# The first weight panel behind a norm, four output tiles advanced chunk by chunk

## The chip, the cores and the metric

The kernel runs on one core of a Trainium2 chip, as one program with five instruction streams: TensorE (PE), VectorE (DVE), ScalarE (ACT), GpSimd (POOL) and SyncE (SP), which order themselves by semaphores. The metric is the device time of one execution in microseconds (us). All data are float32. Three runs of the kernel before took 4790.31, 4792.47 and 4794.86 us, median 4792.47 us.

## The reference, cut to what matters

Two models follow each other over 512 tokens of width 1024. The first has two layers; 256 context tokens run beside the 512 in its first layer and in the mixer of its second. The second has two layers, each with a gated MLP ahead of its mixer and one behind.

```
# first model, each layer
h = modulate(rms_norm(x, g0), sh1, sc1);  x = x + gt1 * rms_norm(mixer(h), g1)
h = modulate(rms_norm(x, g2), sh2, sc2);  x = x + gt2 * rms_norm(square(relu(h @ w1)) @ w2, g3)
# second model, each layer
h = x + 0.5 * swiglu(rms_norm(x, f1), ...)
n = rms_norm(h, mix);  h = h + concat(conv, window attention, memory attention) @ w_out
h = h + 0.5 * swiglu(rms_norm(h, f2), ...);  x = rms_norm(h, final)
swiglu(h) = (silu(h @ w1) * (h @ w3)) @ w2
```

## The kernel before, in words

Activations lie transposed, as eight chunks of 128 features by 512 or 768 tokens (X the residual, H the normed input). Weights come as panels of 8 chunks by 512 columns through a ring of slots that SP fills ahead of use. A panel holds four output tiles of 128 features. An output tile of up to 512 tokens is a sum over eight chunks in one PSUM bank: eight matmuls, each of which the trace records as two weight loads and two matmuls ("passes" below). Output tiles rotate through banks 0 to 3: `tile()` on TensorE (L1069) waits until the tile four back has been read (semaphore `tile_free`), and on VectorE (L2155) until the tile is done (`tile_done`). `columns` (L1084) goes output tile by output tile and, inside, chunk by chunk; for its first tile it waits per chunk for `h_act`, ScalarE's signal that this chunk of H is written.

Seven panels stand right behind a norm:

- In the even mixer of the first model (`even_in`, L1172): four column tiles times two token segments, 512 and 256 wide. ScalarE writes each chunk of H from VectorE's row scaling (L1754). VectorE copies the tiles out and pools them (L2247 to L2271).
- In the two MLPs of the first model (`mlp`, L1315), item up 0 0: segments of 384 and 384 tokens in the first layer, one of 512 in the second. ScalarE applies relu (L1870) and VectorE multiplies (L2459).
- In the four gated MLPs of the second model (`swiglu`, L1392), item up 0 0: the panel's four tiles are a1, b1, a2, b2 (w1 and w3 columns by turns). Here H is X times the norm's gains, and the factor 1/rms of each token (`r_row`) is applied to the product instead. TensorE computes the sum of squares as a product with a matrix of ones, `root` (L1341), between the panel's first and second tile. VectorE has added up the squares before (L2489, L2492), and behind it makes the variance (L2497), ScalarE the root (L1878), VectorE the reciprocal (L2501). In the third gated MLP (layer 1, first) `root` sums two rows at once and `enter_second` (L2510) needs two roots and two reciprocals, since the layer's final norm and the next norm are folded together.

VectorE's order in these four MLPs is written out (L2734): the reciprocal, `right_first` (L2591, four sums over H through L2563, for the next panel), `first_up` (L2723), `left_sums` (L2608, L2616 and L2618, on the next panel's weights), then the next panel's unit. `first_up` takes a1 times `r_row` (L2726), waits for ScalarE's sigmoid (L1971), multiplies (L2729), multiplies by b1 (L2730), and does the same for a2, b2. In the first of the four, `tables` (L3021 to L3040, the rotary angles) stands between the two pairs.

The other panels of the MLPs are computed as seven products of half size in place of eight (`seven`, L1367, through L1363). The unit's first and second products need only a free bank and the panel; the third one issued, `product(6)`, waits for `tile_free` and so for `left_second` on VectorE (L2631), which stands behind `left_sums` and behind ScalarE's copy of the first product (L1944).

Of the kernel before, what the change touches and what calls it, by code (L numbers as in the profile page):

```python
# [15 lines left out]
P = 128  # L16
D = 1024
KD = D // P
LAT = 512
CTX = 256  # L20
TOK = LAT + CTX
# [44 lines left out]
def mlp_order(beside):  # L66

    for step, (kind, g) in enumerate(mlp_steps(len(FF1_GROUPS))):
        for part in range(2):
            if beside and step in MOD_STEPS:  # L70
                yield "mod", 2 * (step - MOD_STEPS[0]) + part, 0
            yield kind, g, part
# [220 lines left out]
def build_program(nc, panels, vecs, consts, x_in, c_in, mem_in, pool_w, bias, pos, window_in, out, x_save):  # L293
    npanels = panels.shape[0]
    with ExitStack() as ctx:
# [5 lines left out]
        def sem(name):  # L301
            if name not in sems:
                sems[name] = ctx.enter_context(nc.semaphore(name))
            return sems[name]
# [16 lines left out]
        def area(at, *shape):  # L321
            n = int(np.prod(shape))
            flat = arena[:, at:at + n]
            if len(shape) == 1:
                return flat
            names = " ".join("abcd"[:len(shape)])
            return flat.rearrange(f"p ({names}) -> p {names}", **{"abcd"[i]: s for i, s in enumerate(shape)})
# [3 lines left out]
        X, H, Y = (area(o, KD, TOK) for o in (X0, H0, Y0))  # L331
# [129 lines left out]
        SEG1 = ((0, LAT),)  # L461
# [405 lines left out]
        def counting():  # L867


            n = defaultdict(int)  # L870

            def more(name, k=1):
                n[name] += k
                return n[name]

            def one(name):
                n[name] += 1
                return 1

            return n, more, one  # L880
# [179 lines left out]
        def _(pe):  # L1060
            n, more, one = counting()

            def panel():
                p = n["panel"]
                n["panel"] += 1
                pe.wait_ge(sem(f"panel{SLOT[p]}"), 16 * LOADS[p])
                return ring[SLOT[p]]

            def tile():  # L1069

                if n["tile"] - 3 > 0:
                    pe.wait_ge(sem("tile_free"), n["tile"] - 3)
                n["tile"] += 1
                return ps[:, (n["tile"] - 1) % 4, :]

            def accumulate(dest, left, right, nk=KD, ready=None):

                for k in range(nk):
                    if ready:
                        pe.wait_ge(sem(ready), more(ready))  # L1080
                    ins = pe.matmul(dest, left(k), right(k), start=(k == 0), stop=(k == nk - 1))  # L1081
                ins.then_inc(sem("tile_done"), one("tile_done"))

            def columns(w, ms, src, segs, nk=KD, ready=None):  # L1084
                for m in ms:
                    for a, b in segs:
                        accumulate(tile()[:, 0:b - a], lambda k: w[:, k, m * P:(m + 1) * P],
                                   lambda k: src[:, k, a:b], nk, ready)
                        ready = None

            def rows(w, lo, width, src, tok, cols, ready=None):

                for t in tok:
                    accumulate(tile()[:, 0:width], lambda k: src[:, k, t * P:(t + 1) * P],
                               lambda k: w[:, k, cols:cols + width], KD, ready)
                    ready = None
# [19 lines left out]
            def strips(w):  # L1116

                bank = tile()
                each = KD // STRIPS
                for part in range(each):  # L1120
                    for strip in range(STRIPS):
                        k = strip * each + part
                        ins = pe.matmul(bank[strip * STRIP:(strip + 1) * STRIP, :], silu_c[:, k, :], w[:, k, :],  # L1123
                                        start=(part == 0), stop=(part == each - 1))
                ins.then_inc(sem("tile_done"), one("tile_done"))
# [14 lines left out]
            def mod(i, lo, hi):  # L1140

                for j in range(lo, hi, 2):
                    for _ in range(2):
                        strips(panel())
                    strip_sums(i, 2)
# [24 lines left out]
                row(hi)  # L1170

            def even_in():  # L1172
                columns(panel(), range(4), H, ((0, LAT), (LAT, TOK)), ready="h_act")
                mod(0, 4, 6)
                columns(panel(), range(4), H, SEG2)
                mod(0, 6, 8)
                columns(panel(), range(4), H, SEG2)
                mod(0, 8, 10)
                rows(panel(), 0, 512, H, range(TOK // P), 0)
                mod(0, 10, 12)  # L1180
                pe.wait_ge(sem("const_in"), 16)
                pe.wait_ge(sem("pool_w"), 16)
                for g in range(4):
                    pe.wait_ge(sem("pooled"), more("pooled"))
                    for a, b in SEG2:
                        accumulate(tile()[:, 0:b - a], lambda k: pool_wb[:, g, :], lambda k: Y[:, 4 + g, a:b], 1)
# [128 lines left out]
            def mlp(segs, beside):  # L1315
                ends = {}
                between = None
                for item in mlp_order(beside):
                    kind, g, part = item
                    w = panel()  # L1320
                    if kind == "mod":
                        strips(w)
                        between = lambda: strip_sums(1, 1)
                        continue
                    src = H if kind == "up" else hidden1[g % 2]
                    if kind == "down" and part == 0:
                        pe.wait_ge(sem("half_hidden"), ends[g][0])
                        pe.wait_ge(sem("tile_free"), ends[g][1])
                    fast = cuts(item, FF1_GROUPS, beside)
                    for at, c in enumerate(fast):  # L1330
                        if at == 0 and (part == 0 or item == ("up", 0, 1)):
                            n["right"] += 4
                        seven(w, src, mlp_left, c, beside and item == ("up", 0, 1), between)
                        between = None
                    if not fast:
                        columns(w, range(4), src, segs, KD, "h_act" if kind == "up" else None)
                    if kind == "up":
                        n["half_hidden"] += 4 * len(fast)
                        ends[g] = n["half_hidden"], n["tile"]

            def root(count):  # L1341

                if n["norm"] > 0:
                    pe.wait_ge(sem("var"), n["norm"])
                n["norm"] += count
                for i in range(count):
                    pe.wait_ge(sem("accumulated"), more("accumulated"))
                    ins = pe.matmul(ps[:, 4 + i, :], ones[:, :], acc[i], start=True, stop=True)
                ins.then_inc(sem("summed"), one("summed"))
# [42 lines left out]
            def swiglu(l, which):  # L1392
                ends = {}
                for item in swiglu_order():
                    kind, g, part = item
                    w = panel()
                    if kind == "down" and part == 0:
                        pe.wait_ge(sem("half_hidden"), ends[g][0])
                        pe.wait_ge(sem("tile_free"), ends[g][1])
                    fast = cuts(item, FF2_GROUPS)  # L1400
                    if fast:
                        if part == 0 or item == ("up", 0, 1):
                            n["right"] += 4
                        seven(w, H if kind == "up" else hidden2[g % 2], ffn_left, fast[0])
                        if (which, g, part, kind) == (0, 0, 0, "down"):
                            mem_root()
                    elif kind == "up":
                        columns(w, [0], H, SEG1, KD, "h_act")
                        root(2 if (l, which) == (1, 0) else 1)
                        columns(w, range(1, 4), H, SEG1)  # L1410
                    else:
                        columns(w, range(4), hidden2[g % 2], SEG1, FF2_GROUPS[g])
                    if kind == "up":
                        n["half_hidden"] += 4 * len(fast)
                        ends[g] = n["half_hidden"], n["tile"]
# [1733 lines left out]
```

## Time and profile before

| what | us |
|---|---|
| median of 3 runs | 4792.47 |
| profiled execution, first to last instruction (span) | 4789.8 |
| TensorE matmuls busy | 4575.2 (96%) |
| VectorE busy | 2702.2 (56%) |
| ScalarE busy | 1044.4 (22%) |

The profiled execution shows its span alone; what lies around it has no row of its own. The span is 2.7 us less than the median. Matmul busy time is modelled and includes time at the lower of the two clocks (1.2 and 2.4 GHz); the mean granted clock over the span is 0.972 of the full one.

### The profile page before, as it was taken

The numbers are of one execution on the slowest core, as the hardware profiler recorded it, in microseconds if no ns is written. First come the engines' busy times: TensorE is split into PE (matmuls) and PEld (weight loads), VectorE is DVE, ScalarE is ACT, GpSimd is POOL, SyncE is SP. The second block draws the span as 40 slices with busy tenths as digits, with TensorE's granted clock in tenths as the row PEclk, the third lists the DMA queues.
The fourth block names the chain that finished last, engine by engine and source line by source line (L and its number), as shares of the span: only waits on it lengthen the run. The fifth ranks groups of instructions, "written<-read, shape, count | busy, mean of one in ns | idle before, by whom it ended". The sixth has DMA issues, their size and how long they took to land.

```text
span 4789.8 us, 70253 instructions
## 1 busy us (share of the span) xinstructions
PE 4575.2 (96%) x29914; PEld 3231.8 (67%) x29914; DVE 2702.2 (56%) x4820; ACT 1044.4 (22%) x2337; POOL 81.2 (2%) x81
## 2 busy tenths in 40 slices
PE   7999999998999999999999999989999999989998
PEld 5556555555536676665886788545887788545886
DVE  3172445534326777744565666674657666674666
ACT  1052100002016666642001110151001010151000
POOL 0000000000000000000000000020000000020000
PEclk9998999998999999998999999989999999989999
DMA  5211122221100000012222122211222222211221
GB/s 234 111 45 53 53 106 106 106 88 53 66 18 3 3 3 3 3 38 99 86 88 91 71 88 79 88 53 70 88 88 80 73 86 80 91 51 71 88 88 44
DMA packets 27046, 339.09 MB, mean 71 GB/s; under 512 B 3024, under 2 KB 3024, under 8 KB 6896
## 3 DMA queue, kind: packets, MB, share of 16 engines
q1 hardware_dynamic: 24048, 324.51, 18.0%
q0 software_dynamic: 2688, 10.09, 0.6%
q8 instruction: 238, 3.90, 0.3%
q14 instruction: 72, 0.59, 0.0%
HBM read 330.40 MB, written 4.19 MB: 70 GB/s over the span
## 4 chain that ended last, share of the span: by engine, by line
PE 88%; DVE 7%; ACT 4%; issue 2%; DMA 0%; SPq 0%; ACTq 0%; DVEq 0%
PE ps L1363 46%; PE ps L1081 23%; PE ps L1153 2%; PE ps L1562 1%; PE ps L1493 1%; PE ps L1545 1%; PE ps L1534 1%; PE ps L1610 1%; PE ps L1123 1%; ACT arena L1803 1%; PE ps L1304 1%; PE ps L1618 1%; PE ps L1431 1%; DVE arena L2875 1%; PE ps L1579 1%
## 5 line engine op out<-in xcount | busy, mean ns | idle before, releaser
L1363 PE MATMUL ps<-arena 128*128 128x256 f32 (+1 forms) x9096 | 2111.8, 394 | 15.1 <-DVE arena L2631 15.1
L1363 PEld LDWEIGHTS ps<-arena 128*128 128x128 f32 x9096 | 1731.3, 191 | 383.3 <-DVE arena L2631 17.5
L1081 PE MATMUL ps<-arena 128*128 128x512 f32 (+3 forms) x3104 | 1152.6, 532 | 10.6 <-ACT arena L1754 7.2
L1081 PEld LDWEIGHTS ps<-arena 128*128 128x128 f32 x3104 | 584.3, 192 | 566.3 <-issue 401.8
L2622 DVE TENSOR_TENSOR arena<-ps,arena 128x512 f32<-128x512 f32 (+1 forms) x250 | 157.6, 630 | 314.6 <-PE ps L1363 312.8
L2622 DVE TENSOR_TENSOR square<-ps,square 128x512 f32<-128x512 f32 (+1 forms) x145 | 99.1, 684 | 176.1 <-PE ps L1363 176.1
L2563 DVE TENSOR_TENSOR arena<-arena 128x1024 f32<-128x1024 f32 (+2 forms) x153 | 190.5, 1245 | 8.7 <-ACT arena L1754 5.5
L1944 ACT COPY square<-ps 128x512 f32<-128x512 f32 (+1 forms) x65 | 37.2, 573 | 658.0 <-PE ps L1363 590.7
L1944 ACT COPY arena<-ps 128x384 f32<-128x384 f32 (+1 forms) x35 | 18.5, 529 | 575.1 <-PE ps L1363 549.2
L2883 DVE COPY_PREDICATED arena<-const,ps 128x256 f32<-128x256 int32 x192 | 83.7, 445 | 79.6 <-PE ps L1562 74.3
L1803 ACT ACTIVATE arena<-arena,state_sum 128x256 f32<-128x256 f32 (+2 forms) x128 | 76.4, 598 | 214.6 <-DVE state_sum L2350 212.6
L1562 PE MATMUL ps<-arena 64*64 64x64 f32 x3072 | 122.3, 222 | 0.8 <-ACT arena L2017 0.5
L2631 DVE TENSOR_TENSOR arena<-arena 128x1024 f32<-128x1024 f32 (+1 forms) x60 | 72.5, 1208 | 89.0 <-ACT square L1944 79.9
L1363 PE MATMUL ps<-arena,square 128*128 128x256 f32 (+1 forms) x432 | 122.0, 431 | 0.0
L2035 ACT COPY arena<-ps 128x256 f32<-128x256 f32 x240 | 87.6, 371 | 156.9 <-PE ps L1534 154.7
L2622 DVE TENSOR_TENSOR reset<-ps,square 128x512 f32<-128x512 f32 (+1 forms) x65 | 43.9, 675 | 135.1 <-PE ps L1363 135.1
L1562 PEld LDWEIGHTS ps<-arena 64*64 64x64 f32 x3072 | 104.1, 134 | 19.3 <-issue 10.9
L1534 PE MATMUL ps<-const,arena 128*128 128x128 f32 x480 | 105.2, 301 | 12.2 <-DVE arena L2883 11.3
L1935 ACT ACTIVATE reset<-arena 128x256 f32<-128x256 f32 x40 | 16.7, 417 | 426.7 <-DVE arena L2696 426.7
L2618 DVE TENSOR_TENSOR arena<-arena 128x1024 f32<-128x1024 f32 (+2 forms) x100 | 107.6, 1076 | 3.4
L2637 DVE TENSOR_TENSOR arena<-arena 128x1024 f32<-128x1024 f32 (+2 forms) x100 | 107.1, 1071 | 1.3
L1363 PEld LDWEIGHTS ps<-arena,square 128*128 128x128 f32 x432 | 82.1, 190 | 33.3
(341 smaller groups left out, 4845.1 us busy)
## 6 DMA issues: line engine op xcount, KB each, us to landing
arena<-in_panels SPq DMA_DIRECT2D x144, 2048.0 KB, 7.8
arena<-in_panels SPq DMA_DIRECT2D x9, 1536.0 KB, 6.3
arena<-in_bias POOLq DMA_DIRECT2D x8, 512.0 KB, 4.5
arena<-in_x_in SPq DMA_DIRECT2D x1, 3072.0 KB, 11.1
x_save<-arena POOLq DMA_DIRECT2D x1, 2048.0 KB, 7.5
arena<-x_save POOLq DMA_DIRECT2D x1, 2048.0 KB, 13.0
out_x<-arena SPq DMA_DIRECT2D x8, 256.0 KB, 2.2
arena<-in_panels SPq DMA_DIRECT2D x1, 1792.0 KB, 11.6
```

Source lines behind the costliest of these rows:

```text
L1081: ins = pe.matmul(dest, left(k), right(k), start=(k == 0), stop=(k == nk - 1))
L1153: ins = pe.matmul(ps[:, 4, 0:TILES], square[:, c % 2, t * P:(t + 1) * P], to_column(t), start=(c == 0 and t == 0), stop=(c == KD - 1 and t ...
L1363: ins = pe.matmul(bank[:, j * cut.side:(j + 1) * cut.side], left[:, k, j * P:(j + 1) * P], right[k], start=(k == 0), stop=(k == cut.rows - 1))
L1534: ins = pe.transpose(dest[:, q * P:(q + 1) * P], flat(xt[t % 2][d][:, q, :, :]), ident)
L1562: ins = pe.matmul(ps[half(h), 2 * d, 2 * P + i * C:2 * P + (i + 1) * C], left[half(h), :], right[half(h), :], start=True, stop=True)
L1803: act.activation(p_h, p_h, ACT.Exp, bias=soft_at(i, h, NEGMAX), scale=-1.0, accum_out=soft_at(i, h, SUM)).then_inc(sem(f"exped{h}"), one(f ...
L2035: act.copy(x_sb[d].rearrange("p a b c -> p (a b c)"), src).then_inc(sem(f"x_ready{d}"), one(f"x_ready{d}"))
L2563: ins = dve.tensor_tensor(part, x[:, rows], y[:, rows], op)
L2618: dve.tensor_tensor(a21, left_block(w, 0, 0, c), a21, ALU.subtract).then_inc(sem("left"), one("left"))
L2622: dve.tensor_tensor(out, product_of(tile(), cut), other, ALU.add).then_inc(sem("tile_free"), one("tile_free"))
L2637: dve.tensor_tensor(a12, a12, a11, ALU.subtract).then_inc(sem("left"), one("left"))
L2883: ins = dve.copy_predicated(z, level_mask(d, level + 1), chunked(ps[:, 2 * d, 2 * P:4 * P]))
```

## The change

A new helper `together` takes the banks of all its output tiles first, then goes chunk by chunk: for each chunk one wait for `h_act`, then one matmul into each bank. It serves the first four tiles of the seven panels above (two column tiles by two segments, or four by one). In the gated MLPs `root` moves from behind the first tile to behind chunk 3 of 8, so behind half of the work of all four tiles. The number of matmuls and the reading of the tiles on ScalarE and VectorE stay as they are.

```diff
+            def together(w, ms, src, segs, ready, halfway=None):
+                banks = [(m, a, b, tile()) for m in ms for a, b in segs]
+                for k in range(KD):
+                    pe.wait_ge(sem(ready), more(ready))
+                    for m, a, b, bank in banks:
+                        ins = pe.matmul(bank[:, 0:b - a], w[:, k, m * P:(m + 1) * P], src[:, k, a:b], start=(k == 0),
+                                        stop=(k == KD - 1))
+                        if k == KD - 1:
+                            ins.then_inc(sem("tile_done"), one("tile_done"))
+                    if k == KD // 2 - 1 and halfway:
+                        halfway()
             def even_in():
-                columns(panel(), range(4), H, ((0, LAT), (LAT, TOK)), ready="h_act")
+                w, segs = panel(), ((0, LAT), (LAT, TOK))
+                together(w, range(2), H, segs, "h_act")
+                columns(w, range(2, 4), H, segs)
             def mlp ...
-                        columns(w, range(4), src, segs, KD, "h_act" if kind == "up" else None)
+                        first = 4 // len(segs) if kind == "up" else 0
+                        if first:
+                            together(w, range(first), src, segs, "h_act")
+                        columns(w, range(first, 4), src, segs)
             def swiglu ...
-                        columns(w, [0], H, SEG1, KD, "h_act")
-                        root(2 if (l, which) == (1, 0) else 1)
-                        columns(w, range(1, 4), H, SEG1)
+                        together(w, range(4), H, SEG1, "h_act", lambda: root(2 if (l, which) == (1, 0) else 1))
```

## Rows read from the trace of the kernel before

**Rows 1.** The page: span, and the chain that ended last by engine.

```profile
span 4789.8 us, 70253 instructions
PE 88%; DVE 7%; ACT 4%; issue 2%; DMA 0%; SPq 0%; ACTq 0%; DVEq 0%
```

**Rows 2.** Windows: length, busy time of PE, PEld, DVE, ACT, POOL, clock, DMA.

```profile
58.16:102.24 44.08, 44.08 (x128) 25.13 (x128) 16.03 (x37) 9.51 (x15) 0.00 (x0) 0.94 0.12 49
483.12:528.27 45.15, 44.21 (x128) 24.79 (x129) 13.73 (x17) 11.66 (x21) 0.00 (x0) 0.96 0.00 0
2218.30:2248.72 30.42, 30.42 (x64) 13.32 (x65) 10.09 (x13) 6.58 (x10) 0.00 (x0) 0.90 0.00 1
2623.11:2657.20 34.09, 30.84 (x67) 13.08 (x68) 28.75 (x40) 15.08 (x23) 1.10 (x2) 0.94 0.04 12
3705.00:3725.60 20.60, 20.60 (x49) 9.12 (x48) 17.47 (x15) 3.56 (x5) 0.00 (x0) 1.00 0.00 0
1166.27:1199.01 32.74, 32.74 (x97) 19.27 (x98) 28.52 (x45) 6.53 (x10) 0.00 (x0) 0.95 0.00 1
```

**Rows 3.** Timeline, first MLP, its norm's last step: start, duration, engine, line [idle before, releaser].

```profile
481.67 9.68 ACT L1754 ACTIVATE arena<-arena,mod,gain 128x512 f32<-128x512 f32 x16 [2.75 <-DVE arena L2215]
```

**Rows 4.** Timeline, first gated MLP, its first panel and what follows.

```profile
2623.11 9.31 PE L1081 MATMUL ps<-arena 128*128 128x512 f32 x16 [2.88 <-ACT arena L1892]
2635.66 1.10 PE L1348 MATMUL ps<-square,ones 128*128 128x512 f32 x2 [3.25 <-DVE stat L2492]
2646.61 0.69 DVE L2726 TENSOR_TENSOR arena<-ps,rstd 128x512 f32<-128x512 f32 x1
2649.40 0.42 DVE L3030 CAST arena<-arena 128x512 f32<-128x512 int32 x1
2656.30 0.69 DVE L2726 TENSOR_TENSOR arena<-ps,rstd 128x512 f32<-128x512 f32 x1
2659.09 1.22 DVE L2616 TENSOR_TENSOR arena<-arena 128x1024 f32<-128x1024 f32 x1
2661.70 1.22 DVE L2631 TENSOR_TENSOR arena<-arena 128x1024 f32<-128x1024 f32 x1
```

**Rows 5.** Timeline, third gated MLP, around its first panel.

```profile
3696.62 0.69 DVE L2422 TENSOR_TENSOR arena<-ps,arena 128x512 f32<-128x512 f32 x1 [0.40 <-PE ps L1081]
3703.29 1.88 PE L1348 MATMUL ps<-square,ones 128*128 128x512 f32 x4
3716.66 5.00 DVE L2563 TENSOR_TENSOR arena<-arena 128x1024 f32<-128x1024 f32 x4
3721.70 0.69 DVE L2726 TENSOR_TENSOR arena<-ps,rstd 128x512 f32<-128x512 f32 x1
3727.27 1.22 DVE L2616 TENSOR_TENSOR arena<-arena 128x1024 f32<-128x1024 f32 x1
```

**Rows 6.** Timeline, second gated MLP, and the fourth's product with ones.

```profile
3291.14 0.69 DVE L2390 TENSOR_TENSOR arena<-ps,arena 128x512 f32<-128x512 f32 x1 [6.17 <-PE ps L1081]
3297.81 1.02 PE L1348 MATMUL ps<-square,ones 128*128 128x512 f32 x2
3319.26 26.06 PE L1363 MATMUL ps<-arena 128*128 128x256 f32 x120
...
4373.15 1.02 PE L1348 MATMUL ps<-square,ones 128*128 128x512 f32 x2
```

**Rows 7.** TensorE's waits: total us, times, longest.

```profile
PE ps L1363 <- DVE arena L2631: 15.1, 5, 4.8
```

**Rows 8.** Timeline: TensorE behind one of those waits.

```profile
2838.00 19.22 PE L1363 MATMUL ps<-arena 128*128 128x256 f32 x80 [4.52 <-DVE arena L2631]
```

**Rows 9.** Windows behind two of those waits, and behind 3.25 us of idling.

```profile
2635.66:2657.20 21.54, 21.54 (x51) 9.58 (x52) 17.00 (x20) 6.43 (x8) 0.00 (x0) 1.00 0.00 1
2838.00:2850.00 12.00, 12.00 (x48) 10.28 (x49) 5.55 (x6) 0.00 (x0) 0.00 (x0) 0.86 0.00 1
3809.96:3822.00 12.04, 12.04 (x45) 10.21 (x46) 6.20 (x9) 0.42 (x1) 0.00 (x0) 0.80 0.01 1
```

## The prediction

> **What bounds the kernel now.** I read the page's chain first: 88% of the span hangs on TensorE, 7% on VectorE [rows 1]. So work taken off TensorE counts only where TensorE waits for it, and a delay on VectorE counts from the point where TensorE comes to need it. Next the windows over the first panels, to see how much of each was waiting and how much the lower clock. Between 3705.00 and 3725.60 TensorE ran 48 passes of 512 columns at the full clock: 20.60 / 48 = 0.429 us each. A stretch's length times its granted clock, less its passes times 0.429, is the time waited [rows 2]. Last the timelines of the gated MLPs, which show what VectorE does between the product with ones and the next panel's third product [rows 4 to 6].
>
> **What the change removes.**
>
> Even mixer: 64 passes of 512 and 64 of 256 are 96 full ones, 41.2 us; the window gives 44.08 x 0.94 = 41.4. Only 0.2 us was waiting; for the rest of the first tile the clock was at its lower level, and TensorE no faster than ScalarE [rows 2]. First MLP: 128 passes of 384 are 41.2 us, the window gives 45.15 x 0.96 = 43.3: 2.1 us of waiting, which goes, since four tiles of a chunk cost TensorE 8 x 0.322 = 2.6 us, while ScalarE gives a chunk of H each 9.68 / 8 = 1.2 us [rows 3]. Second MLP: 64 passes are 27.5 us, the window 30.42 x 0.90 = 27.4: no waiting, no gain. First gated MLP: 66 passes are 28.3 us, the window 34.09 x 0.94 = 32.2 [rows 2]: 3.8 us, of which 3.25 is the wait for the squares' sum ahead of `root` [rows 4]. With `root` behind 32 passes that sum, ready at 2635.5, is long there at about 2638.7. In the other three gated MLPs TensorE goes without a gap from its last projection or down tile into the panel and through `root`: nothing to gain.
>
> On TensorE alone: 0.2 + 2.1 + 3.8 = 6.1 us.
>
> Alternating four banks and four weight tiles costs little: the odd mixer's first panel does it already, 96 passes of 384 in 32.74 x 0.95 = 31.1 us against 96 x 0.322 = 30.9 [rows 2]. Bounds: 0 to 0.2 us per panel; I take 0.
>
> **What it adds (1): all four banks at once.** `together` asks for its fourth bank before its first matmul, so it waits for the tile just finished to be read. In the first, second MLP and first gated MLP the norm has emptied all banks long before. In the second gated MLP the panel began at 3297.81 - 16 x 0.429 = 3290.94; the last read ends at 3291.14 + 0.69 = 3291.83, and with 0.13 us for the signal (squares' sum to matmul) the start is 3291.96 [rows 6]. That is 1.0 us; the third, 3703.29 - 6.87 = 3696.42 against 3696.62 + 0.69 + 0.13 = 3697.44, gives 1.0 as well [rows 5], and the fourth repeats the second's rows. Together 3.0 us.
>
> **What it adds (2): the chain behind `root` comes later, and the four tiles finish together.** Before, VectorE worked on a1 and b1 while TensorE still computed a2 and b2. Now all four end within the last 3 x 0.86 = 2.6 us, and `root` stands 32 passes in and not 16, 6.9 us later. Behind the panel TensorE has two products, 2 x 3.43 = 6.9 us (16 passes of 256 each), before `product(6)` needs `left_second`.
>
> From the first L2726 to L2616 VectorE needs 3727.27 - 3721.70 = 5.6 us where nothing stands between the pairs [rows 5]; from L2616 to the end of L2631 it needs 2661.70 + 1.22 - 2659.09 = 3.8 us [rows 4]. Sum 9.4 us.
>
> - Second and fourth gated MLP: from `root` to the end of L2563, where `first_up` starts, there are 2646.61 - 2635.66 = 11.0 us [rows 4]. With `root` 13.7 us into the panel, `r_row` and H's sums are there 24.7 us in; the first tile is done at 28.3 - 2.6 = 25.7. So the tiles decide. A tile's read starts 0.2 us behind it (3290.94 to 3291.14), so VectorE ends L2631 at 25.7 + 0.2 + 9.4 = 35.3 us, TensorE reaches `product(6)` at 28.3 + 6.9 = 35.2. With the signal 0.3 us each: 0.6 us.
> - First gated MLP: the panel starts at 2623.1, loses 34.09 x 0.06 = 1.9 us to the lower clock [rows 2] and ends at 2653.3, where it ended at 2657.2. But `tables` stands between the pairs: 2656.30 - 2649.40 = 6.9 us [rows 4], before hidden behind a2 and b2. VectorE starts at 2653.3 - 2.4 = 2650.9 and ends L2631 at 2650.9 + 5.6 + 6.9 + 3.8 = 2667.3. `product(6)` starts at 2667.4 and not at 2657.20 + 6.86 = 2664.1. The 3.8 us gained become a loss of 3.4, with TensorE idle from 2660.2 for 7.2 us.
> - Third gated MLP: `root` at 3697.4 + 13.7 = 3711.2; from `root` to L2563 there are 3716.66 - 3703.29 = 13.4 us (two roots, two reciprocals), then 5.0. `first_up` starts at 3729.6, not 3721.7 [rows 5]. TensorE is through at 3697.4 + 29.2 = 3726.6 and waits 3.8 us for the first bank; `left_second` ends at 3729.6 + 9.4 = 3739.0. `product(6)` starts at 3739.1; before it was 3725.60 + 6.87 = 3732.5. Loss 6.6 us, the 1.0 for the bank in it.
>
> Even mixer, both first MLPs: each tile's read depends on nothing late, and the next product needs the first bank at least 1.7 us after it was done, against one or two operations of up to 0.69 us to read it. The pooling behind the even mixer's last column tile waits for that tile, which ends last as before, so its distance to TensorE stays. Queues: `root` passes no panel wait; SP's loads wait for the count of finished tiles, which is complete when it was; POOL waits for nothing here.
>
> The Trainium skill (Perfetto Trace Analysis, section Optimizing Tensor Performance, Matmuls) says that independent groups should rotate through banks so that reading one overlaps computing the next. It speaks against this change, which opens all four and closes them together; by it the three late chains are the rule and not an accident. It names no price, so the sum is without it.
>
> **What it adds (3): the clock behind the new waits.** TensorE waited for L2631 five times, 15.1 us in all [rows 7], once 4.5 us up to 2838.00 [rows 8]. Behind two such waits the clock was 0.86 and 0.80 over 12 us: 12 x 0.14 = 1.7 us and 12.04 x 0.20 = 2.4 us lost. Behind the 3.25 us wait before `root` it stayed at 1.00 [rows 9]. The first gated MLP's 7.2 us: 1.7 to 3.0 (30.42 x 0.10, the loss at a start out of long idling [rows 2]), I take 2.0. The third's 3.8 and 1.8 us lie near both kinds: 0 to 4.8, I take 1.0.
>
> **The sum.** Gains 0.2 + 2.1 = 2.3. Losses: first gated MLP 3.4 + 2.0, second and fourth 2 x 1.0 + 0.6, third 6.6 + 1.0: 15.6. Net 13.3 us slower. The profiled span 4789.8 becomes 4803.1; the median stands 2.7 above that span, so 4805.8 us, +0.28%. About 0.2% (9.6 us) is what a measurement of this kernel tells from no change.
>
> **The rivals.**
> 1. *VectorE is hidden after all.* If TensorE did not need `left_second` so early, or VectorE started on the tiles sooner than I count, only the banks' 3.0 us stand against 6.1: 4789.4, not slower. For it: VectorE is busy 56% on average, and 6.9 us of products lie ahead of the need. Against it: the third MLP's chain would have to be 5.6 us shorter, and its durations are read off. It decides where L2631 ends within 6.9 us of the panel's end in all four.
> 2. *Waits as computed, clock untouched.* 10.3 us: 4802.8, and some microseconds less if waits overlap better. For it: the 3.25 us case. Against it: the 4.5 us case.
> 3. *The clock falls more often.* 3.0 and 4.8 us in place of 2.0 and 1.0, plus 0.2 a panel: 4812. For it: the third MLP idles twice within 9 us.
>
> **How the numbers follow.** Forecast (4803 to 4810) 0.60; rival 1 0.14; rival 2 (4798 to 4803) 0.14; rival 3 0.12. Slower by over 0.2%: forecast and rival 3 whole, a little of rival 2, 0.73; within 0.2%: 0.24, rival 1 and most of rival 2; faster by over 0.2% would need 9.6 us where TensorE has 6.1 to give: 0.03. Range 4797 to 4812: it leaves out rival 1 and the upper end of rival 3.
>
> **What would show it.** Right: in the first gated MLP no idle before L1348, and 7 us of TensorE waiting for VectorE behind the second product; in the third about 4 and 2 us; in the second and fourth 1 us ahead of the first pass; in the first MLP 2 us less up to its first L1363. Wrong: `product(6)` of the first gated MLP earlier than 2664 less the 2.3 us gained before, or `first_up` of the third at its old distance from the panel's end.

## The result and the profile after

| | us, median | runs |
|---|---|---|
| before | 4794.86 (4790.31 to 4798.34) | 9 |
| changed | 4806.01 (4801.27 to 4808.89) | 9 |

The ratio is 1.0024, with a 95% interval of 1.0015 to 1.0033: the change makes the kernel 11 us slower (7 to 16), where 13.3 were forecast. The profiled execution went from a span of 4789.8 to 4803.9 us, 14.1 us.

First the page of the changed kernel, which answers to [rows 1].

```profile
span 4803.9 us, 70267 instructions
PE 87%; DVE 8%; ACT 3%; issue 2%; DMA 0%; SPq 0%; ACTq 0%; DVEq 0%
```

One per cent of the chain has gone from TensorE to VectorE. The passes of `together` stand under L1090, of `seven` under L1381, `root` under L1366; on VectorE L2579, L2742, L2632 and L2647 are what L2563, L2726, L2616 and L2631 were. The windows over the same four panels (length, busy times, granted clock, DMA), against [rows 2]:

```profile
56.41:97.86 41.45, 41.45 (x128) 24.21 (x128) 15.84 (x37) 9.52 (x15) 0.00 (x0) 1.00 0.15 63
479.67:523.46 43.79, 43.79 (x128) 25.64 (x129) 13.73 (x17) 11.67 (x21) 0.00 (x0) 0.94 0.00 0
2216.76:2246.89 30.13, 30.13 (x65) 13.15 (x66) 9.41 (x12) 6.58 (x10) 0.00 (x0) 0.91 0.00 1
2621.56:2651.54 29.98, 29.98 (x66) 13.25 (x67) 22.20 (x29) 12.13 (x19) 1.10 (x2) 0.95 0.05 14
```

Length times clock is now 41.5, 41.2, 27.4 and 28.5 us, the passes' own 41.2, 41.2, 27.5 and 28.3. Before they were 41.4, 43.3, 27.4 and 32.2. The clock is printed to two places, so each product is good to 0.2 us. Within that, all waiting inside the first MLP's and the first gated MLP's panels is gone, and the even mixer's has not changed: that its panel is 2.6 us shorter is the clock, 1.00 for 0.94. Changing bank and weights with every matmul costs nothing that these rows show. The same is seen directly at the full clock in the third gated MLP, where the kernel before runs 32 passes tile by tile (first line) and the changed one runs 32 chunk by chunk (second line), both in 13.90 us:

```profile
3689.55 13.90 PE L1081 MATMUL ps<-arena 128*128 128x512 f32 x32
3717.53 13.90 PE L1090 MATMUL ps<-arena 128*128 128x512 f32 x32
```

The other side is in what TensorE waits for before L1381 (releaser, us in total, times), against [rows 7]:

```profile
  DVE arena L2647: 22.1, 6
  DVE arena L2742: 3.6, 1
```

The timeline of the first gated MLP, against [rows 4] (start, duration, engine, line, idle before):

```profile
2621.56 15.55 PE L1090 MATMUL ps<-arena 128*128 128x512 f32 x32 [2.88 <-ACT arena L1908]
2636.95 1.02 PE L1366 MATMUL ps<-square,ones 128*128 128x512 f32 x2
...
2649.24 0.69 DVE L2742 TENSOR_TENSOR arena<-ps,rstd 128x512 f32<-128x512 f32 x1 [1.45 <-PE ps L1090]
...
2658.93 0.69 DVE L2742 TENSOR_TENSOR arena<-ps,rstd 128x512 f32<-128x512 f32 x1
...
2664.33 1.23 DVE L2647 TENSOR_TENSOR arena<-arena 128x1024 f32<-128x1024 f32 x1
...
2665.61 24.65 PE L1381 MATMUL ps<-arena 128*128 128x256 f32 x105 [7.00 <-DVE arena L2647]
```

No idle time stands before L1366 any more. VectorE reads the first tile at 2649.24, when all four are nearly done; the tables fill the time up to 2658.93, and TensorE stands still for 7.00 us ahead of the third product.

The third gated MLP, against [rows 5]:

```profile
3702.00 13.97 PE L1090 MATMUL ps<-arena 128*128 128x512 f32 x32 [0.98 <-DVE arena L2438]
3715.81 1.88 PE L1366 MATMUL ps<-square,ones 128*128 128x512 f32 x4
...
3734.23 0.69 DVE L2742 TENSOR_TENSOR arena<-ps,rstd 128x512 f32<-128x512 f32 x1
3734.95 0.63 ACT L1987 ACTIVATE square<-arena 128x512 f32<-128x512 f32 x1 [8.61 <-DVE arena L2742]
3735.07 15.21 PE L1381 MATMUL ps<-arena 128*128 128x256 f32 x56 [3.64 <-DVE arena L2742]
```

TensorE waits 0.98 us for the banks, then 3.64 us until VectorE frees the first bank: its `first_up` starts 18.4 us behind `root` as before, but `root` is 6.9 us later. The second gated MLP, against [rows 6]:

```profile
3294.95 13.97 PE L1090 MATMUL ps<-arena 128*128 128x512 f32 x32 [0.98 <-DVE arena L2406]
...
3330.50 1.59 PEld L1381 LDWEIGHTS ps<-arena 128*128 128x128 f32 x8 [0.48 <-DVE arena L2647]
```

The clock behind the two long waits, against [rows 9]:

```profile
3735.07:3744.87 9.80, 9.80 (x32) 8.12 (x33) 6.95 (x8) 1.73 (x3) 0.00 (x0) 0.70 0.31 130
2665.61:2677.61 12.00, 12.00 (x48) 10.30 (x49) 6.78 (x9) 0.42 (x1) 0.00 (x0) 0.85 0.00 0
```

9.80 x 0.30 = 2.9 us and 12.00 x 0.15 = 1.8 us are lost. These clocks are means over the stretch: in windows of 1 us the clock was 0.50 (1.2 GHz) up to 3740.9 and 1.00 (2.4 GHz) from there. It had fallen at about 3734.1, before TensorE went on.

To sum a gated MLP up in one number I take the distance between two events that hang on TensorE in every variant: from the last transposes of the norm (first MLP) or the reading of the last tile ahead of the panel (others) to ScalarE's copy of the first product in the unit after the next. Differences to the kernel before, in us, worked out from the timelines, with the change of the clock's loss inside in brackets (length times what the clock lacks to 1.00, summed over 40 short windows of the same stretch):

| gated MLP | distance before | changed | forecast for it |
|---|---|---|---|
| first | 65.55 | +5.17 (3.4) | +5.4 |
| second | 56.03 | +1.57 (0) | +1.3 |
| third | 56.89 | +7.98 (3.4) | +7.6 |
| fourth | 56.03 | +1.56 (0) | +1.3 |
| sum | | +16.3 | +15.6 |

The bracket can't simply be taken off: a slow clock costs nothing while TensorE would otherwise stand waiting for VectorE.

With the 2.3 us forecast for the first model this gives 14.0, and the spans differ by 14.1. That they agree so well is partly luck. TensorE comes to the first gated MLP only 1.8 us ahead (2617.71 against 2619.55), and 1.75 us of that were there before the first panel. The even mixer's and the first MLP's panels are 4.0 us shorter, but the two stretches between the panels, where both kernels do the same, are 4.2 us longer (381.81 for 380.88 and 1693.30 for 1690.03), with 6.4 us more lost to the clock in short windows.

### The profile page after: what moved, and what is told of

It reads as the page before. It is cut to its first block, busy times and chain, and to the rows that moved or that the text cites. A ratio compares the mean times of both kernels' runs of the same rounds, so it can differ in the third digit from the quotient of the medians.

```text
span 4803.9 us, 70267 instructions
## 1 busy us (share of the span) xinstructions
PE 4580.7 (95%) x29914; PEld 3238.5 (67%) x29914; DVE 2702.5 (56%) x4820; ACT 1045.4 (22%) x2337; POOL 81.2 (2%) x81
## 4 chain that ended last, share of the span: by engine, by line
PE 87%; DVE 8%; ACT 3%; issue 2%; DMA 0%; SPq 0%; DVEq 0%; ACTq 0%
PE ps L1381 45%; PE ps L1081 19%; PE ps L1090 3%; PE ps L1166 2%; PE ps L1578 1%; PE ps L1509 1%; PE ps L1561 1%; PE ps L1550 1%; PE ps L1626 1%; PE ps L1136 1%; ACT arena L1819 1%; PE ps L1319 1%; PE ps L1634 1%; PE ps L1447 1%; DVE arena L2891 1%
## 5 line engine op out<-in xcount | busy, mean ns | idle before, releaser
L1381 PE MATMUL ps<-arena 128*128 128x256 f32 (+1 forms) x9096 | 2117.4, 395 | 25.9 <-DVE arena L2647 22.1
L1381 PEld LDWEIGHTS ps<-arena 128*128 128x128 f32 x9096 | 1734.4, 191 | 396.9 <-DVE arena L2647 25.9
L1081 PE MATMUL ps<-arena 128*128 128x512 f32 (+3 forms) x2656 | 959.7, 522 | 0.4 <-DVE arena L2386 0.4
L1090 PE MATMUL ps<-arena 128*128 128x512 f32 (+1 forms) x448 | 187.5, 579 | 12.2 <-ACT arena L1770 6.3
L2579 DVE TENSOR_TENSOR arena<-arena 128x1024 f32<-128x1024 f32 (+2 forms) x153 | 190.5, 1245 | 8.7 <-ACT arena L1770 5.4
L1090 PEld LDWEIGHTS ps<-arena 128*128 128x128 f32 x448 | 87.3, 196 | 110.3 <-issue 102.0
L1381 PE MATMUL ps<-arena,square 128*128 128x256 f32 (+1 forms) x432 | 122.0, 431 | 0.0
L2647 DVE TENSOR_TENSOR arena<-arena 128x1024 f32<-128x1024 f32 (+1 forms) x60 | 72.4, 1207 | 87.0 <-ACT square L1960 77.5
L1578 PEld LDWEIGHTS ps<-arena 64*64 64x64 f32 x3072 | 104.7, 135 | 19.5 <-issue 8.8
L2634 DVE TENSOR_TENSOR arena<-arena 128x1024 f32<-128x1024 f32 (+2 forms) x100 | 107.6, 1076 | 3.4
```

What stands on the lines that cost most here:

```text
L1090: ins = pe.matmul(bank[:, 0:b - a], w[:, k, m * P:(m + 1) * P], src[:, k, a:b], start=(k == 0), stop=(k == KD - 1))
L1381: ins = pe.matmul(bank[:, j * cut.side:(j + 1) * cut.side], left[:, k, j * P:(j + 1) * P], right[k], start=(k == 0), stop=(k == cut.rows - 1))
L1578: ins = pe.matmul(ps[half(h), 2 * d, 2 * P + i * C:2 * P + (i + 1) * C], left[half(h), :], right[half(h), :], start=True, stop=True)
L2579: ins = dve.tensor_tensor(part, x[:, rows], y[:, rows], op)
L2634: dve.tensor_tensor(a21, left_block(w, 0, 0, c), a21, ALU.subtract).then_inc(sem("left"), one("left"))
```

## The experiments

Each kernel ran beside the kernel before on the same chip. My theory was that of the prediction: TensorE's passes cost the same in either order, and the loss is VectorE's chain behind the product with ones, which comes later and whose tiles are done all at once. The rivals were that the new order itself costs TensorE time, that the tiles ending together alone or the place of the product alone is harmful, and that the lower clock is the cause of the loss and not what follows from the waits.

**e1: the new order only in the first model.**

```diff
-                        together(w, range(4), H, SEG1, "h_act", lambda: root(2 if (l, which) == (1, 0) else 1))
+                        columns(w, [0], H, SEG1, KD, "h_act")
+                        root(2 if (l, which) == (1, 0) else 1)
+                        columns(w, range(1, 4), H, SEG1)
```

> The even mixer and the two MLPs of the first model keep the new order, the four gated MLPs go back to the old one with the product with ones behind the first tile. Theory (the loss is VectorE's chain in the gated MLPs coming later, TensorE's passes cost the same in either order): 2.3 us faster than the kernel before, all of it waiting removed in the first two places, of which 2.1 in the first MLP between its first pass and its first L1363 after the clock is taken out. Rival (changing the bank and the weights at each chunk costs TensorE time, so the new order loses everywhere): the three panels take longer than their passes times 0.429 us at the granted clock, and the kernel is not faster, 0 to 4 us slower.

Measured: 4792.66 us against 4794.48, ratio 0.9996 (0.9987 to 1.0005). The time can't tell 2 us from nothing, and the spans of the two profiled executions don't show it either (4791.5 against 4789.8). The windows can. The first MLP's panel in a window:

```profile
482.53:526.81 44.28, 44.28 (x128) 25.80 (x129) 13.72 (x17) 11.66 (x21) 0.00 (x0) 0.93 0.00 0
```

44.28 x 0.93 = 41.2 us, 2.1 less than before, as in the changed kernel. The four gated MLPs have the distances of before, but the first, which has 2.0 more, 1.7 of it the clock. The rival that the order costs TensorE time has no row for it, and the 13.90 us of 32 passes in either order speak against it.

**e2: the new order only in the gated MLPs.**

```diff
-                w, segs = panel(), ((0, LAT), (LAT, TOK))
-                together(w, range(2), H, segs, "h_act")
-                columns(w, range(2, 4), H, segs)
+                columns(panel(), range(4), H, ((0, LAT), (LAT, TOK)), ready="h_act")
...
-                        first = 4 // len(segs) if kind == "up" else 0
-                        if first:
-                            together(w, range(first), src, segs, "h_act")
-                        columns(w, range(first, 4), src, segs)
+                        columns(w, range(4), src, segs, KD, "h_act" if kind == "up" else None)
```

> Only the four gated MLPs have the new order, the first model's three panels are as before. Theory: about 15.5 us slower than the kernel before, more than the whole change's own 11 to 14, split as 3 to 5 in the first, 1.4 in the second and in the fourth, 7 to 8 in the third. Rival (order costs TensorE time everywhere): less than the whole change, since three of seven panels are left as they were.

Measured: 4808.74 us against 4794.48, ratio 1.003 (1.0019 to 1.0041): 14.3 slower (9 to 20), by the medians no less than the whole change with its 11 (7 to 16); that it is more, the times don't show. Distances: +5.1, +1.6, +6.8, +1.6, sum 15.0, the first and third just outside what was expected of them. The loss is all in the gated MLPs.

**e10: the product with ones moved, and nothing else.**

```diff
-                        columns(w, [0], H, SEG1, KD, "h_act")
+                        columns(w, [0, 1], H, SEG1, KD, "h_act")
                         root(2 if (l, which) == (1, 0) else 1)
-                        columns(w, range(1, 4), H, SEG1)
+                        columns(w, range(2, 4), H, SEG1)
```

> The kernel before, tile by tile, with one edit: in the gated MLPs the product with ones stands behind the second tile and not behind the first, 6.9 us later, as far into the panel as in the changed kernel. No bank is taken early and no tiles end together. Theory (the place of the product with ones sets VectorE's start, in the third MLP by itself): third MLP 5.5 us slower plus 0 to 3 for the clock; first MLP about 2 us slower plus up to 2 for the clock, since the wait for the squares goes but the rotary tables now stand behind the later start; second and fourth unchanged. Sum 7 to 12 us slower than before. Rival (the four tiles ending together are what counts, the product's place is harmless): third MLP unchanged, first MLP 3 us faster, sum 3 us faster.

Measured: 4799.87 us against 4794.48, ratio 1.0012 (1.0003 to 1.0021), 5.4 us slower; in the profile +4.8, 0, +6.5, 0, sum 11.3, with 3.4 us more lost to the clock in each of the two; the first is above the 2 to 4 expected of it. The timeline of TensorE in the first and third gated MLP:

```profile
2669.07 11.16 PE L1363 MATMUL ps<-arena 128*128 128x256 f32 x40 [5.59 <-DVE arena L2631]
...
3736.76 13.43 PE L1363 MATMUL ps<-arena 128*128 128x256 f32 x49 [3.64 <-DVE arena L2726]
```

The third MLP's wait of 3.64 us is there to the hundredth without any tiles ending together and without banks taken early. In the first a wait of 5.59 us appears as well. The rival that the product's place is harmless is out. The profile's 11.3 us lies in the expected 7 to 12; the time, 5.4 us (1 to 10), has its middle below that, and only the upper end of its interval reaches in. The profiled execution was one of the long ones (4804.32 us, 4.5 above the median), so its clock losses may be more than usual. How much of the whole loss the product's place makes by itself is therefore known only roughly.

**e3: the product with ones back behind 16 passes, tiles still together.** `after` is a new argument of `together`, the number of chunks ahead of the product, 4 where nothing is given.

```diff
-                    if k == KD // 2 - 1 and halfway:
+                    if k == after - 1 and halfway:
...
+                                 2 if (l, which) == (1, 0) else 2)
```

> The changed kernel with the product with ones behind two chunks, 16 passes, in all four gated MLPs: as far into the panel as in the kernel before. Theory: the third MLP's wait for the first bank goes and so does the slow clock behind it, 7 us less there; in the first MLP TensorE waits 3.5 to 4 us for the squares again and everything behind moves by that; second and fourth unchanged. Net 3 to 4 us faster than the changed kernel, 8 to 11 us slower than the kernel before. Rival (in the third MLP the four tiles' ending together costs what was seen): the third MLP keeps 7 us and the whole is 3 to 4 us slower than the changed kernel.

Measured: 4807.07 us against 4794.06, ratio 1.0031 (1.0019 to 1.0042), 13.0 slower (9 to 20) where 8 to 11 were expected, and not 3 to 4 faster than the changed kernel but 2 slower by the medians, which the noise doesn't tell from the same. Distances: +11.5, +1.6, +1.6, +1.6, sum 16.2. TensorE's timeline, and VectorE's first read in the first gated MLP:

```profile
2633.98 1.42 PE L1366 MATMUL ps<-square,ones 128*128 128x512 f32 x2 [3.98 <-DVE stat L2509]
2635.20 22.18 PE L1090 MATMUL ps<-arena 128*128 128x512 f32 x48
...
2654.91 0.69 DVE L2743 TENSOR_TENSOR arena<-ps,rstd 128x512 f32<-128x512 f32 x1 [9.69 <-PE ps L1090]
...
2657.21 7.07 PE L1381 MATMUL ps<-arena 128*128 128x256 f32 x32
2671.28 14.03 PE L1381 MATMUL ps<-arena 128*128 128x256 f32 x54 [7.00 <-DVE arena L2648]
...
3737.68 12.60 PE L1381 MATMUL ps<-arena 128*128 128x256 f32 x56
```

The third MLP gave back 6.4 of its 8.0 us: there it is the product's place. The first has both waits, 3.98 us for the squares and the same 7.00 us for L2648, which is L2631 before. VectorE stood 9.69 us waiting for the first tile. So there the tiles' end decides and not the product, as the prediction had it (first read at 2650.9, while `root` at 2638.7 plus 11.0 us gives 2649.7). The first cost 6.3 us more than in the changed kernel: 3.98 are the wait, 1.7 the clock behind it, which I had not put there (12.00 us from there ran at 0.86). e3 and e10 together say that in the first MLP either edit alone makes VectorE late, since the 6.9 us of tables stand behind both.

**e4: the product with ones behind six chunks.**

```diff
-                    if k == KD // 2 - 1 and halfway:
+                    if k == after - 1 and halfway:
...
+                                 6 if (l, which) == (1, 0) else 6)
```

> The changed kernel with the product with ones behind six chunks and not four, 6.9 us later again. Theory: VectorE's start is set by it in all four gated MLPs now: third product of the next panel 6.9 us later in the third MLP, 5 to 6 in the others, so 22 to 24 us slower than the changed kernel and 34 to 42 slower than the kernel before, with 0 to 5 of it the clock. Rival (tiles ending together decide): no change in the first, second and fourth MLP, where the first tile ends 25.7 us in: at most 7 us slower than the changed kernel.

Measured: 4830.09 us against 4794.48, ratio 1.0072 (1.006 to 1.0085): 35.6 slower and 24 more than the changed kernel, as expected. Distances +11.9, +8.1, +14.1, +7.0, so 6.7, 6.5, 6.1 and 5.5 more than changed, with 1.7 to 3.4 us more lost to the clock in each. The second gated MLP, quiet so far, now waits for the first bank too:

```profile
3333.66 26.51 PE L1381 MATMUL ps<-arena 128*128 128x256 f32 x109 [3.90 <-DVE arena L2743]
```

Counted from the panel's first pass, VectorE's `first_up` starts 6.9, 5.5, 6.9 and 5.5 us later than in the changed kernel (in the third 3753.88 - 3714.79 against 3734.23 - 3702.00). Two chunks are 6.9 us. The second and fourth take off their slack, the 1.37 and 1.45 us for which VectorE waited for the first tile in the changed kernel; the first had 1.45 us too, but lost as much to the slower clock inside the panel. The rival, no change in these three, is out.

**e5: the rotary tables out of the way.**

The edit on VectorE; ScalarE's own `tables()` moves alike, to ahead of its square root.

```diff
                 for c in range(KD):
                     add_square(1, 0, c)
+                if name == "ffn1_norm0":
+                    tables()
                 variance(r_row, ps[:, 4, :])
...
-                    if (l, which, c) == (0, 0, 0):
-                        tables()
```

> The changed kernel, with the rotary tables of the first gated MLP moved on VectorE and ScalarE from between the two pairs of tiles to ahead of the variance, where VectorE waits about 4 us for the product with ones. Theory (the tables between the pairs are what turned the first MLP's gain into a loss): the wait of 7 us for L2647 there shrinks to 1 to 2.5 us, the clock does not fall behind it, and the kernel is 5 to 7 us faster than the changed one, so 5 to 8 us slower than the kernel before. Rival (the wait has another cause, the panel's late end or ScalarE's copy): the wait stays over 5 us and the time within 2 us of the changed kernel's.

Measured: 4798.06 us against 4794.06, ratio 1.0011 (1.0001 to 1.002): 4.0 slower (0 to 10), 7 less than the changed kernel. The middle lies just under the 5 to 8 expected against the kernel before; by the spans it is 7.4. TensorE in the first gated MLP, and the window behind it:

```profile
2660.07 20.12 PE L1381 MATMUL ps<-arena 128*128 128x256 f32 x92 [1.38 <-DVE arena L2649]
```

```profile
2660.07:2672.07 12.00, 12.00 (x56) 10.59 (x57) 8.11 (x12) 0.48 (x2) 0.00 (x0) 1.00 0.01 1
```

7.00 us of waiting became 1.38, and the clock stayed up: the first MLP's distance is 2.2 us below that of the kernel before. The other three are as in the changed kernel. Of the 3.7 us of waiting that the new order took out of this panel, 2.2 now come through. The rest is the wait of 1.38 us, and the tables are still part of it: `root` ends at 2637.03 + 1.02 = 2638.05, but VectorE is at the tables until 2640.76 and takes up the variance only then.

```profile
2637.03 1.02 PE L1366 MATMUL ps<-square,ones 128*128 128x512 f32 x2
2640.79 0.69 DVE L2513 TENSOR_SCALAR rstd<-ps 128x512 f32<-128x512 f32 x1
```

**e6: banks taken one by one.**

```diff
-                banks = [(m, a, b, tile()) for m in ms for a, b in segs]
+                banks = [[m, a, b, None] for m in ms for a, b in segs]
...
-                    for m, a, b, bank in banks:
+                    for entry in banks:
+                        if k == 0:
+                            entry[3] = tile()
+                        m, a, b, bank = entry
```

> The changed kernel, but each bank is taken right before its first matmul and not all four ahead of the first. Theory: the 0.98 us in front of the panel goes in the second, third and fourth gated MLP, all else stays at its distance, 2.9 us faster than the changed kernel, 9 to 11 slower than the kernel before. Rival (the start does not matter because VectorE's chain decides where TensorE goes on): the idle time moves to the third product and the time stays.

Measured: 4799.3 us against 4794.06, ratio 1.0012 (1.0003 to 1.0021), 5.2 slower (1 to 10) where 9 to 11 were expected; by the spans 7.5. Distances +5.2, +0.35, +5.6, +0.34: 1.2 us less in the second and fourth than in the changed kernel, and 2.4 less in the third, where 1.0 was expected. The third:

```profile
3698.70 13.90 PE L1093 MATMUL ps<-arena 128*128 128x512 f32 x32
3712.43 1.88 PE L1369 MATMUL ps<-square,ones 128*128 128x512 f32 x4
3714.15 13.90 PE L1093 MATMUL ps<-arena 128*128 128x512 f32 x32
3731.68 7.15 PE L1384 MATMUL ps<-arena 128*128 128x256 f32 x32 [3.64 <-DVE arena L2745]
3740.31 9.98 PE L1384 MATMUL ps<-arena 128*128 128x256 f32 x45 [1.48 <-DVE arena L2650]
```

```profile
3731.68:3743.68 12.00, 10.52 (x48) 8.97 (x49) 9.20 (x11) 2.15 (x4) 0.00 (x0) 1.00 0.27 113
```

The 0.98 us are gone and nothing took their place. The third MLP shows something besides: the same 3.64 us wait, and this time the clock stays at 1.00. Then the second wait that the prediction named appears, 1.48 us; in the changed kernel the slow clock had stretched the two products so far that `left_second` was done before them. So here is the loss without the clock: 5.6 us, and 6.6 with the 0.98 for the banks. This puts the rival of the clock as the cause out; in the changed kernel's third MLP it adds 8.0 - 6.6 = 1.4 us.

**e8 and e9: two ways to keep the gain.** e8 is e5 and e6 together, with the product with ones behind two chunks in the third gated MLP alone.

```diff
-                        together(w, range(4), H, SEG1, "h_act", lambda: root(2 if (l, which) == (1, 0) else 1))
+                        together(w, range(4), H, SEG1, "h_act", lambda: root(2 if (l, which) == (1, 0) else 1),
+                                 2 if (l, which) == (1, 0) else 4)
...
-                    if k == KD // 2 - 1 and halfway:
+                    if k == after - 1 and halfway:
```

> The changed kernel with three repairs together: the rotary tables ahead of the variance in the first gated MLP, the product with ones behind two chunks in the third (four in the others), each bank taken right before its first matmul. Theory, from the single edits: against the kernel before the first gated MLP 2.2 us less, the second, third and fourth 0.3 to 0.6 more each, the first model's three panels 2.3 less: 3 to 4 us faster than the kernel before, 14 to 16 faster than the changed one. Rival (the edits hide one another, or the clock falls as often as before): the third MLP keeps a wait of over 3 us, and the kernel stays slower than the one before.

e9 takes the new order only where TensorE had waited: the first model, and the first gated MLP with the tables ahead as in e5.

```diff
+                        if (l, which) == (0, 0):
+                            together(w, range(4), H, SEG1, "h_act", lambda: root(1))
+                        else:
+                            columns(w, [0], H, SEG1, KD, "h_act")
+                            root(2 if (l, which) == (1, 0) else 1)
+                            columns(w, range(1, 4), H, SEG1)
```

> The new order only where TensorE waited: the first model's three panels and the first gated MLP, the latter with the rotary tables ahead of the variance; the other three gated MLPs as in the kernel before. Theory: 2.3 and 2.2 us less and nothing more elsewhere, 4 to 5 us faster than the kernel before. Rival (what is taken out of a wait is given back in the clock or behind it): within 2 us of the kernel before.

Measured: e8 4788.88 us, e9 4789.5 us, before 4794.43; both ratios 0.9989 (0.998 to 0.9998). Distances: e8 -1.9, +0.35, +0.34, +0.35; e9 -2.1, 0, 0, 0. Both beat the kernel before by 5 us (1 to 10) and the changed one by some 16. Expected were 3 to 4 us for e8 and 4 to 5 for e9. Which is the better is open: the times can't tell, the distances favour e9 by 1.3 us, the spans of the profiled executions (4783.7 and 4786.8) favour e8. In e8 the clock was low for longer at the start of the first gated MLP (5.0 us lost in its stretch against 3.4 in e9), the panel began 4.9 us behind the last transposes and not 3.8, and so VectorE had more time for the tables: no wait is left at all, where e9 has 1.41 us:

```profile
2661.96 3.29 PE L1381 MATMUL ps<-arena 128*128 128x256 f32 x14 [1.41 <-DVE arena L2654]
```

## Why the prediction was right, step by step

- *Waiting removed, 6.1 us.* The windows give 43.3 to 41.2 in the first MLP and 32.2 to 28.5 in the first gated one: 5.8 us. The even mixer's 0.2 us did not show. e1 shows the first MLP's part by itself in its window; in the time it is within the noise. The prediction's 32.2 does not come out of the product written there: 34.09 x 0.94 is 32.0. Short windows give 1.9 us lost to the clock in that stretch, and so 32.2.
- *No cost of the alternating order.* Held in all four windows.
- *Banks, 3 x 1.0 us.* 0.98 us three times; e6 removed them with nothing in their place.
- *First gated MLP, a gain turned into a loss of 3.4.* The third product began 44.05 us behind the panel's first pass (2665.61 - 2621.56) where it took 40.95 (2657.20 + 6.86 = 2664.06, less 2623.11): 3.1 us. The forecast's own terms, 2667.4 - 2664.1, make 3.3. `first_up` began at 27.7 us and the forecast was 27.8. e5 shows the tables as the part that decides.
- *Third gated MLP, 6.6 us.* The wait of 3.64 us was forecast as 3.8; the second wait of 1.8 us showed as 1.48 in e6. e10 and e3 pin it on the product's place, from both sides.
- *Second and fourth, 0.3 us beside the banks.* It was 0.6: TensorE's weight load waits 0.48 us for L2647. VectorE ended L2647 35.5 us into the panel (3329.23 + 1.23 - 3294.95) and not 35.3; the rest of the difference lies between its signal and TensorE's next products, for which the forecast had 0.2 us.
- *The clock, 2.0 and 1.0 us.* It took 1.8 us in the first. In the third 2.9 were lost, but the slow products hid the second wait, so that the clock added 1.4 and the whole comes to 8.0 and not 7.6. The range for it was right; that the chosen 1.0 lay near is luck, since nothing in the rows would have named the value: e6 has the same wait with no loss.
- *The rivals.* VectorE hidden (4789) came out nowhere; e9 gets a gain only by leaving three panels alone and taking the tables out of the chain. The clock falling more often (19.5 us, 4812) lies outside the interval of 7 to 16. The clock untouched (10.3 us) does not: by the time alone it fits as well as the forecast, and it is the windows at 0.85 and 0.70 that speak against it.

The forecast of 4805.8 stood on a median of 4792.47 from three runs; nine gave 4794.86. The change itself was put at 13.3 us and measured at 11 (7 to 16) by time, 14.1 by the two profiles. That the absolute figure fell within 0.2 us is luck: the base was 2.4 us too low and the change 2.1 too high. The 2.7 us between span and median in the forecast were not one thing either: each later execution took 1.8 us more than its span (4805.67 against 4803.9), and the profiled execution (4789.8 + 1.8 = 4791.6) was 0.9 below the median. What the runs leave open is how much of the difference between single executions is the clock falling at other places: before the first panel, where the two kernels do the same, the profiles already differ by 1.8 us.

## What to carry to other kernels

An order that opens all output tiles of a panel and closes them together removes waits for the input chunk by chunk, but it also takes away the time in which the first tiles are read, so ask for each use whether TensorE waited there and what the reading engine has to do before the next product. A small product in the middle of a long run (here the sum of squares) sets the start of a whole chain on another engine: place it by the time its result is needed, and not by the time its input is ready. Work tucked between two reads (here the tables) is free only as long as the reads have slack; move it before changing what gives that slack.

## What the runs showed of the hardware

One and the same idle time of TensorE had different effects on its clock. Five kernels have the wait of 3.64 us ahead of the first product behind the third gated MLP's panel, with the same products behind it. The clock fell to 1.2 GHz in four of them: over the next 10 to 12 us it was 0.70 on the mean in the changed kernel (9.80 us) and in e5, 0.78 in e10, 0.83 in e2. In e6 it stayed at 1.00. After 3.25 us in the kernel before it stayed at 1.00 too [rows 9], after 3.98 us in e3 it was 0.86. Up to 3.0 us were lost behind a wait of that length, or nothing, and where the slow stretch covered another wait only part of the loss reached the time: 1.4 us in the changed kernel. This alone moves single executions by as much as the smaller steps here.
